# One 3 MB load for each expert in the loop over the turns, and one wait for each joined load

## What is computed

```python
def _moe(x2d, w_router, router_bias, w_gate, w_up, w_down, ws_gate, ws_up, ws_down):
    scores = jax.nn.sigmoid((x2d @ w_router).astype(jnp.float32))
    ...
    _, idx = lax.top_k(jnp.where(emask, choice, -jnp.inf), TOP_K)      # 8 of 64 experts for each token
    ...
    def body(y, blk):
        tok, gate, e = blk
        xb = x2d[tok]
        h = jax.nn.silu(xb @ w_gate[e]) * (xb @ w_up[e])
        out = (h @ w_down[e]) * gate[:, None].astype(x2d.dtype)
        return y.at[tok].add(out), None
    ...
    shared = (jax.nn.silu(x2d @ ws_gate) * (x2d @ ws_up)) @ ws_down
    return routed + shared
```

## Time and profile before

| | us |
|---|---|
| median of 3 runs | 745.39 |
| lowest and highest run | 743.74, 745.47 |
| the profiled execution | 744.41 |
| its span, first to last instruction | 742.5 |

### The profile page before, as it was taken

The page is one execution under the profiler, slowest core; times in us unless marked ns, Lnnn a source line. Parts: engine busy times, 40 slices in busy tenths (PEclk is TensorE's granted clock), DMA queues, the critical chain, the costliest instruction groups (busy, mean ns, idle before and its releaser), DMA issues.

```text
span 742.5 us, 11168 instructions
## 1 busy us (share of the span) xinstructions
PE 715.2 (96%) x4520; PEld 416.7 (56%) x4520; DVE 260.8 (35%) x639; ACT 164.9 (22%) x345; POOL 48.0 (6%) x65
## 2 busy tenths in 40 slices
PE   7999999999999999999999999999998999999993
PEld 6888888888864455444444445444443445444441
DVE  3401599656757085222112121022211122112225
ACT  1010423407950043211211111111111121111111
POOL 0120020320320020100000000000000000000000
PEclk9999999999999999999999999999999999999998
DMA  8963544544399548999999999999999999999993
GB/s 329 408 210 147 173 169 167 175 169 159 125 375 376 226 160 332 359 391 423 428 418 429 423 432 429 433 426 421 434 425 422 427 430 419 429 425 421 417 405 157
DMA packets 30931, 250.98 MB, mean 338 GB/s; under 512 B 4001, under 2 KB 4785, under 8 KB 10017
## 3 DMA queue, kind: packets, MB, share of 16 engines
q1 hardware_dynamic: 27792, 240.78, 79.3%
q0 software_dynamic: 2432, 8.44, 3.3%
q10 hardware_dynamic: 656, 1.05, 0.5%
HBM read 249.27 MB, written 1.11 MB: 337 GB/s over the span
## 4 chain that ended last, share of the span: by engine, by line
PE 77%; DVE 9%; SPq 6%; DMA 6%; issue 1%; ACT 1%; DVEq 0%
PE bank L1194 22%; PE bank L820 16%; PE bank L1262 9%; PE bank L1112 8%; PE bank L963 7%; DMA arena<-in_we_dram 5%; PE bank L1132 5%; DVE arena L1585 5%; SPq L627 3%; PE bank L934 1%; PE bank L900 1%; SPq L636 1%; PE bank L1236 1%; PE bank L1271 1%; ACT bank L1350 1%
## 5 line engine op out<-in xcount | busy, mean ns | idle before, releaser
L1194 PE MATMUL bank<-arena 128*64 128x512 f32 (+2 forms) x1008 | 198.7, 601 | 3.7 <-DMA arena<-in_we_dram 3.7
L820 PE MATMUL bank<-arena 128*128 128x256 f32 x768 | 167.7, 379 | 0.0
L820 PEld LDWEIGHTS bank<-arena 128*128 128x128 f32 x768 | 145.6, 190 | 20.5 <-issue 0.4
L1194 PEld LDWEIGHTS bank<-arena 128*64 128x64 f32 (+2 forms) x1008 | 57.7, 127 | 95.6 <-issue 92.9
L1262 PE MATMUL bank<-arena 128*64 128x512 f32 (+2 forms) x512 | 91.7, 584 | 3.3 <-DMA arena<-in_we_dram 1.8
L1112 PEld LDWEIGHTS bank<-onehotb,h_part 128*128 128x128 bf16 x1248 | 69.9, 98 | 20.1 <-issue 20.0
L1112 PE MATMUL bank<-onehotb,h_part 128*128 128x128 bf16 x1248 | 74.3, 219 | 0.2 <-DVE onehotb L1815 0.2
L1903 DVE TENSOR_TENSOR y_lo<-bank,y_hi 128x512 fp32r<-128x512 f32 (+1 forms) x51 | 34.7, 680 | 101.8 <-ACT y_hi L1495 75.5
L1880 DVE TENSOR_REDUCE arena<-bank 64x1 f32<-64x3 f32 (+1 forms) x64 | 10.1, 158 | 160.4 <-PE bank L1212 159.8
L1262 PEld LDWEIGHTS bank<-arena 128*64 128x64 f32 (+1 forms) x512 | 26.2, 124 | 53.7 <-issue 44.6
L963 PE MATMUL bank<-arena 128*128 128x512 f32 x128 | 55.3, 592 | 0.0
(11 more groups left out here) (274 smaller groups left out, 489.8 us busy)
## 6 DMA issues: line engine op xcount, KB each, us to landing
arena<-in_we_dram SPq DMA_DIRECT2D x82, 1024.0 KB, 17.9
arena<-in_we_dram SPq DMA_DIRECT2D x17, 3072.0 KB, 30.2
arena<-in_we_dram SPq DMA_DIRECT2D x22, 2048.0 KB, 30.7
arena<-in_wc_dram SPq DMA_DIRECT2D x15, 1024.0 KB, 11.4
arena<-in_wn_dram SPq DMA_DIRECT2D x8, 1024.0 KB, 4.7
arena<-in_wo_dram SPq DMA_DIRECT2D x8, 1024.0 KB, 4.8
apart<-in_we_dram SPq DMA_DIRECT2D x7, 1024.0 KB, 27.9
arena<-decay_rows POOLq DMA_DIRECT2D x5, 1024.0 KB, 7.1
```

Source lines behind the costliest of these rows:

```text
L820: mm = nc.tensor.matmul(bank[n % 2][:, j * S:(j + 1) * S], wk, xk, start=(k == 0), stop=(k == KD - 1))
L1194: mm = nc.tensor.matmul(bank[0][rows[q], :], hc[v][:, k, rows[q]], place[at_q[part][q]][:, c:c + 512], start=(k == 0), stop=(k == KD - 1))
```

## The change

It has three parts. (1) In the turns, outside the closing batch, `loads_of` now gives one load of three thirds for each expert, as the written-out batches from 10 on have. (2) `given_back` and `user` record for each third which third last held its place and when PE gives that back. (3) For a joined load SP no longer waits for each of its places but only for the one that PE gives back last (in the turns for up to two, since a first turn follows other batches than a later one does).

```diff
@@ loads_of
             if closes(b, turn) or (turn is None and b < PAIRED_FROM):
                 return [[(part, q)] for part in range(PARTS) for q in range(w)]
-            if turn is not None or b < WHOLE_FROM:
+            if turn is None and b < WHOLE_FROM:
                 return [[(0, q), (1, q)] for q in range(w)] + [[(2, q)] for q in range(w)]
             return [[(part, q) for part in range(PARTS)] for q in range(w)]
+        given_back, user = {}, {}
@@ take
                 spot[(turn is None, b) + third] = (at_c, fills[at_c], first, signals[first])
+                given_back[(turn is None, b) + third] = user.get(at_c, (-1, -1, -1))
+
+                last = b + (shared(b, turn) == 0) + (0 if turn is None else FIRST_B)
+                user[at_c] = (last, *third)
...
+        def waits_for(b, turn, parts, q):
+
+            if turn is None:
+                return [max(parts, key=lambda p: given_back[True, b, p, q])]
+            return sorted({max(parts, key=lambda p: given_back[at, b, p, q]) for at in (False, None)})
@@ load_batch
-                    for p, _ in whole[::-1]:
-                        if turn is not None or uses(b, turn, p, q):
-                            sp.wait_ge(free[home(b, turn, p, q)], uses(b, turn, p, q))
+                    for p in waits_for(b, turn, [p for p, _ in whole], q):
+                        sp.wait_ge(free[home(b, turn, p, q)], uses(b, turn, p, q))
```

More of the change, by code:

```diff
@@ L523, in build @@
                 take(0, b, whole)
+        for b in range(TURN_B):
+            for load in order[False, b]:
+                for third in load:
+                    at_c = spot[(False, b) + third][0]
+                    given_back[(None, b) + third] = user[at_c]
+                    user[at_c] = (b + FIRST_B + TURN_B, *third)
         for part in range(PARTS):
```

## The result

| | before | after |
|---|---|---|
| median, us | 745.47 (9 runs) | 749.71 (9 runs) |
| lowest and highest run | 743.74, 746.64 | 747.36, 751.62 |
| the profiled execution | 744.41 | 749.71 |
| its span | 742.5 | 747.9 |

The ratio is 1.0051, with a 95% interval from 1.0035 to 1.0067: the changed kernel is slower by half a per cent. The forecast was 749.6 us.

The account below looks back on a forecast made before the run. The stream of weights was taken to set the end, with PE arriving only a little early. Stall 3.7 + clock 1.7 - slack 1.2 = 4.2 us on 745.4 gave 749.6 us, with an 8 in 10 range of 746.3 to 751.0.

Parts of the forecast that it names:

- The slack, 1.2 us: In the closing batch's down part PE idles 0.75 and 0.44 us; a PE later by D moves the end by D - 1.2.
- Fewer waits on SP, worth 0: Dropping SP's waits for already free places saves tens of nanoseconds, hidden behind the DMA queue: worth 0.
- The better rate, 0.8 us over 24 MB: Turn batches 0 to 2: 3 MB loads at 429 instead of 423 GB/s bring batch 2's weights 0.8 us earlier.
- a fixed cost of 2.0 us for each DMA: Trainium skill's rule: 13 loads fewer worth up to 26 us without overlap; the prediction said the trace doesn't agree.
- The new stall, 3.7 us before turn batch 2: PE waits for the fourth expert's joined load, landing last, and starts at 668.0 instead of 664.34; range 2.9 to 4.5 us.
- the signs named: Idle spell of 3 to 4.5 us before turn batch 2; turn batches 3 and 4 start 4 to 5.5 us later, without waits.
- The clock, 1.7 us: After the stall in turn batch 2 PE's clock falls, as in batch 17, costing 1.70 us; range 0 to 1.7.
- The floor in turn batches 3 and 4, 2.0 and 0.4 us: Joined loads would stall these batches 2.0 and 0.4 us, not added to batch 2's stall, since a late PE finds them landed.
- The later give-backs, worth 0: Place 17, for the closing batch's first load, comes free later, at 683.3; queued weights still cover 13.8 us: costs 0.
- The sum: Whole kernel: 3.7 stall + 1.7 clock - 1.2 slack = 4.2 us slower; 748.6 us profiled, 749.6 against the median.
- Rival B: The stall before turn batch 2 comes but the clock holds: cost 2.5 us, 747.9 us; chance 0.20.
- Rivals C and D: C, chance 0.13: end stays with DMA stream, 744.0 to 746.5 us; D, 0.05: DMA queue runs dry before closing batch, 754.6.

Follow-up runs that it names:

- experiments in 6: Kernel before with small matmuls in front of turn batch 4: 18, 745.69 us; 72, 747.95 us. Changed kernel, last expert in thirds, written-out batches too: 746.72 us.
- the clock kept up: Changed kernel with 48 small matmuls, results overwritten, on PE before the wait for weights of turn batch 2: 747.71 us, ratio 1.0032.
- the kernel before with the longer demand: Kernel before, loads unchanged, but PE waits for turn batch 2's four down parts too before its first gate and up matmul: 750.69 us, ratio 1.0070.
- the width-2 kernel: Changed kernel with joined loads only in the turn's width-2 batches, the old loads in turn batch 2: 749.25 us, ratio 1.0043.
- experiment 5: Small matmuls on PE during the wait: 48 before turn batch 2 in the changed kernel, 747.71 us; 56 before turn batch 3, only width-2 batches joined, 748.07 us.

## Why the prediction was right, point by point

**What bounds the kernel.** Right: the stream of weights sets the end with a small slack for PE (experiments in 6). (The 417 to 434 GB/s hold from slice 19 on; slice 18 has 391 in the earlier trace rows. Nothing rests on it.)

**The slack, 1.2 us.** Too small: 1.7 us were absorbed. The closing batch's first gate and up matmuls start 7.0 us later than before (720.05 against 713.06), as turn batch 3 does (687.70 against 680.71 in the earlier trace rows), the last down matmuls only 5.3 us later (734.41 against 729.09 in the earlier trace rows). The traces with 4.0 us of extra work and with the clock kept up lose the same 1.7 us on this stretch. The prediction's two waits, 0.75 and 0.44 us, are in it. The third, of 0.63 us, gave 0.2 us, since PE now waits 0.58 us for DVE in its place; that this wait costs almost nothing was right. The other 0.3 us are small gaps: 0.2 in the closing batch's gate and up part, 0.1 beside the two waits. By the times alone (2.5 us of 4.0, 1.4 to 3.7) a slack of 1.2 isn't excluded.

**Fewer waits on SP, worth 0.** Right within the noise (1.0006, 0.9992 to 1.0019).

**The better rate, 0.8 us over 24 MB.** Right in sign; its size isn't resolved. From the start of batch 17 to the landing that releases turn batch 2 it is 669.65 - 565.79 = 103.9 us, and before from 564.34 to 639.69 + 29.0 = 668.7 it was 104.4: 0.5 us. But other executions with joined loads took 102.8 (with the clock kept up) and 103.9 us (with the old waits), and the kernel before with the longer demand 104.8. The prediction's sentence on a fixed cost of 2.0 us for each DMA rests on a section of the Trainium skill's page "DMA: Bandwidth & Descriptors" that is headed for DMAs issued from GpSimd; these come from SP. In the full queue of the kernel before, loads of 1 MB land 2.4 to 2.5 us apart and loads of 2 MB 4.9 us, so nothing near 2 us comes on top of the bytes of each.

**The new stall, 3.7 us before turn batch 2.** The mechanism is right and its place exact; the size was too small. Two of the signs named were missed by little: the idle spell is 2.71 us and not 3 to 4.5, and turn batch 3 starts 7.0 us later and not 4 to 5.5. Here the prediction used the wrong measure. The idle time depends on when PE arrives (2.40 to 4.81 us in the executions with this wait), and PE arrived late in this execution: batch 17 began 1.45 us later than before, in code whose loads the change doesn't alter, and its first 20 matmuls took 7.50 us instead of 6.21. None of that second part reaches the end, since PE then waits for the landing anyway. What reaches it is the landing itself: turn batch 2 starts at 669.78, 5.4 us after the 664.34 of the earlier trace rows. Taking 1.45 us of these for the stream's lateness in this execution leaves 4.0 us for the change. This split is an estimate from one pair. Over all traces the four with joined loads in turn batch 2 start it at 668.9 to 669.8 (669.2 in the mean), and four in which nothing holds PE there (the kernel before, the one with the new waits alone, the two with PE made late) do so at 663.5 to 665.5 (664.6): 4.6 us, just above the forecast's range of 2.9 to 4.5.

**The clock, 1.7 us.** Right for this execution: 6.20 us where 4.4 to 4.5 are usual. In other executions a fall took 1.4 to 3.0 us.

**The floor in turn batches 3 and 4, 2.0 and 0.4 us, which doesn't add.** It doesn't add (no wait in either batch of the changed kernel). Its size was wrong: 4.06 us in the width-2 kernel. The step took off 1.0 us for a better rate, and there the load landed not earlier but at 684.3, later than the 683.6 of the earlier trace rows, while PE was ready 0.4 us earlier. This too is one execution.

**The later give-backs, worth 0.** Right: 422 GB/s from 683 to 697 us, no dip in front of the closing batch.

**The sum.** On the profiled execution 4.2 us were forecast and 5.3 measured (749.71 - 744.41): 1.45 for the stream's lateness, 4.0 for the landing, 1.7 for the clock, less 1.7 of slack and 0.15 for small waits that fell away within turn batch 2. Between the medians it is 4.2 us, as forecast; the terms as measured give 4.0 + 1.7 - 0.15 - 1.7 = 3.9 us, and with 4.6 for the landing 4.5, both within the interval of 2.6 to 5.0 us. That the forecast came within 0.1 us is luck: the landing was taken 0.3 to 0.9 us too small and the slack 0.5 us too small, the two work against each other, and the interval is 2.4 us wide. Rival B (the clock holds) is what experiment 5 made: 747.7 us against 747.9 forecast. Rivals C and D didn't happen.

## What to carry to other kernels

When a full DMA stream feeds a consumer, the size of a load matters less than the position in the stream of the last byte that the next step waits for: put what is needed first ahead, and never tie it to bytes that are needed later. A consumer's lateness before a landing costs nothing, lateness after it costs everything beyond its slack, so size a new stall from the landing and not from the idle time in one trace. A stall of a few microseconds on TensorE has to be priced with the slow matmuls behind it, which here were a third to a half of the cost.

## What the hardware did that was not expected

The price of a wait isn't a function of its length. Eight executions had an idle spell of 3.19 to 3.23 us before batch 17. The 20 matmuls behind it took 5.97 to 6.21 us in six of them, 7.50 in one (the changed kernel's), and 4.51 in the last, where the clock held:

```profile
565.55 4.51 PE L1214 MATMUL bank<-arena 128*64 128x512 f32 x20 [3.23 <-DMA arena<-in_we_dram]
```

The longest spell before batch 17, 4.38 us in the kernel with the new waits alone, cost the least of the falls there (5.87 us for the 20 matmuls, 1.4 more than 4.51). After 2.40 and 2.71 us before turn batch 2 the clock fell as well, after 1.00 and 1.29 us it didn't.

The cost of a fall differs between executions of the same kernel, and the mean granted clock of each run shows that this reaches the time. In the changed kernel five runs with 0.987 took 749.54 to 751.62 us (750.3 in the mean) and four with 0.991 took 747.36 to 749.96 (748.3). It isn't all of the spread: with the old waits eight of nine runs have 0.987, and they lie 3.8 us apart. Nor is the changed kernel's spread of 4.3 us unusual: the kernel before, with 22 to 31 runs, spreads over 3.9 to 4.4 us.
